# Hybrid SGU and sparse-attention block: the PV result copied in four quarter pieces and added on GpSimd before it is turned

## What is computed

```python
qi, ki, wi -> idx_score; top-256 keys per query row, chunk-causal
scores = einsum('bqhd,bqkd->bhqk', q, k_sel) * scale - slopes * |q - k|
p = softmax(where(valid, scores, NEG))
y = einsum('bhqk,bqkd->bqhd', p, v_sel)              # 8 heads of 64, one shared k and v
ob = rmsnorm(y.reshape(b, s, 8, 64), gb)
mixed = concat([oa * silu(a_z), ob * silu(b_z)])
x = x + einsum('bse,ed->bsd', mixed, w_out)
```

## Time and profile before

| | |
|---|---|
| median of 3 runs | 593.01 us (591.93 to 594.25) |
| the profiled execution: own time, span | 593.83 us, 592.0 us |
| PE busy | 560.3 us, 95% |
| DVE, ACT, POOL busy | 448.8, 372.1, 158.1 us |
| mean granted PE clock | 0.983 |

### The profile page before, as it was taken

The page is one execution under the profiler, slowest core; times in us unless marked ns, Lnnn a source line. Parts: engine busy times, 40 slices in busy tenths (PEclk is TensorE's granted clock), DMA queues, the critical chain, the costliest instruction groups (busy, mean ns, idle before and its releaser), DMA issues.

```text
span 592.0 us, 9061 instructions
## 1 busy us (share of the span) xinstructions
PE 560.3 (95%) x3038; PEld 478.4 (81%) x3038; DVE 448.8 (76%) x1134; ACT 372.1 (63%) x711; POOL 158.1 (27%) x252
## 2 busy tenths in 40 slices
PE   8999999999999999999997987999989899999987
PEld 7997888788788888878886876778878788888876
DVE  4885878998789989998792568888787878657631
ACT  5866777669976767889873546646545455555510
POOL 2750000124299966662200002012020010102020
PEclk9999999999999999999997996999989999999999
DMA  8723100112311121212122352020202001020122
GB/s 232 251 73 90 35 19 20 35 55 89 106 51 40 37 54 37 90 37 55 53 77 84 102 182 90 19 81 28 90 19 86 22 29 46 16 72 2 37 70 71
DMA packets 39981, 39.68 MB, mean 67 GB/s; under 512 B 6144, under 2 KB 28160, under 8 KB 39936
## 3 DMA queue, kind: packets, MB, share of 16 engines
q1 hardware_dynamic: 38896, 39.11, 21.8%
q10 hardware_dynamic: 1040, 0.00, 0.1%
HBM read 30.72 MB, written 8.39 MB: 66 GB/s over the span
## 4 chain that ended last, share of the span: by engine, by line
PE 76%; DVE 15%; ACT 3%; issue 3%; POOL 1%; DMA 1%; DVEq 0%; POOLq 0%; ACTq 0%
PE ps_proj L1041 37%; PE ps_proj L1207 11%; PE ps_proj L1177 5%; PE ps_lg L1069 5%; PE ps_lg L1068 5%; PE ps_tp L1162 4%; PE ps_lg L1207 2%; DVE w_lo L1347 2%; DVE cand L1439 2%; PE ps_tp L1200 1%; DVE lo_f L1648 1%; PE ps_lg L1018 1%; DVE rank L1428 1%; DVE xT_lo L1658 1%; PE ps_tp L1058 1%
## 5 line engine op out<-in xcount | busy, mean ns | idle before, releaser
L1041 PE MATMUL ps_proj<-w_hi,xT_hi 128*128 128x512 f32 (+1 forms) x432 | 165.1, 382 | 2.1 <-DVE w_lo L1347 2.1
L1041 PE MATMUL ps_proj<-w_lo,xT_hi 128*128 128x512 f32 (+1 forms) x432 | 161.8, 375 | 0.0
L1041 PE MATMUL ps_proj<-w_hi,xT_lo 128*128 128x512 f32 (+1 forms) x432 | 161.6, 374 | 0.0
L889 ACT ACTIVATE ps_lg<-score,cand 128x768 f32<-128x768 f32 (+2 forms) x96 | 95.9, 999 | 10.2 <-DVE cand L1439 10.2
L1041 PEld LDWEIGHTS ps_proj<-w_hi,xT_hi 128*128 128x128 f32 x432 | 81.9, 190 | 15.5 <-DVE w_lo L1347 3.1
L1041 PEld LDWEIGHTS ps_proj<-w_lo,xT_hi 128*128 128x128 f32 x432 | 81.8, 189 | 15.1
L1041 PEld LDWEIGHTS ps_proj<-w_hi,xT_lo 128*128 128x128 f32 x432 | 82.0, 190 | 12.3
L943 ACT CAST xT_hi<-ps_tp 128x512 fp32r<-128x512 f32 (+3 forms) x96 | 43.9, 483 | 69.6 <-PE ps_tp L1162 69.3
L1658 DVE TENSOR_TENSOR xT_lo<-ps_tp,xT_hi 128x512 fp32r<-128x512 f32 (+3 forms) x96 | 50.8, 553 | 35.0 <-ACT xT_hi L943 34.6
L711 POOL TENSOR_TENSOR yz<-hi_f,lo_f 128x512 f32<-128x512 f32 x8 | 10.3, 1286 | 189.8 <-DVE hi_f L1675 142.1
L1162 PE MATMUL ps_tp<-ident,lo_f 128*128 128x128 f32 x288 | 45.1, 279 | 10.8 <-DVE hi_f L1675 6.1
(11 more groups left out here) (173 smaller groups left out, 1127.1 us busy)
## 6 DMA issues: line engine op xcount, KB each, us to landing
stage<-in_w_in_dram SPq DMA_DIRECT2D x48, 256.0 KB, 2.7
x_in<-in_x_dram SPq DMA_DIRECT2D x8, 512.0 KB, 5.8
lo_f<-in_x_dram SPq DMA_DIRECT2D x7, 512.0 KB, 4.1
out_dram<-lo_f SPq DMA_DIRECT2D x7, 512.0 KB, 3.5
q_scratch<-nat SPq DMA_DIRECT2D x8, 256.0 KB, 2.0
q_in<-q_scratch SPq DMA_DIRECT2D x8, 256.0 KB, 3.5
stage<-in_w_out_dram SPq DMA_DIRECT2D x8, 256.0 KB, 2.6
z_scratch<-nat SPq DMA_DIRECT2D x8, 256.0 KB, 2.0
```

The lines of the kernel that those rows point to most:

```text
L889: act.activation(ps_lg[i % 2][:, 0:keys(t)], score[:, sc_off[t]:sc_off[t] + keys(t)], ACT.Sign, bias=cand[:, t:t + 1].bitcast(F32), scale= ...
L1041: mm = pe.matmul(ps_proj[u % 2][:, 0:n], a[:, k, rows], b[:, k, 0:n], start=(k == 0 and i == 0), stop=(k == KB - 1 and i == 2))
```

## The change

The copy becomes four: for odd and even heads and for the high and the low half, 64 partitions by 256 columns each, so that head pairs lie on 128 partitions. POOL adds the two halves (`add_parts`), and PE transposes two head pairs with the identity, 128 columns each, in place of four `fold` matmuls of 64. `fold` goes. `STEPS` moves one output block from h = 6 to h = 5, ahead of `turn_y`, and `mT` stands ahead of the (now no) blocks of h = 6.

```diff
-        yT = place("yT", [P, 4, P], F32, at=top[0])
+        yT = place("yT", [P, 2, P], F32)
+        y_parts = place("y_parts", [P, 2, 2, P], F32, at=top[0])
-            pool.tensor_tensor(fold[:, :], ident[:, 0:DH], ident[:, DH:P], ALU.add).then_inc(fold_ready, 1)
-            for t in range(T):
+            def add_parts(t, half):
+
+                n = 2 * t + half
+                pool.wait_ge(y_parts_done, n + 1)
+                if n > 0:
+                    pool.wait_ge(yT_done, n)
+                pool.tensor_tensor(yT[:, :, :], y_parts[:, 0, :, :], y_parts[:, 1, :, :],
+                                   ALU.add).then_inc(yT_added, 1)
+
+            for t in range(T):
+                add_parts(t, 0)
+                add_parts(t, 1)
                 finish_b(t)
-            def copy_yT(t, half):
+            def split_y(t, half):
 
                 n = 2 * t + half
                 act.wait_ge(pv_done, 2 * (n + 1))
                 if n > 0:
-                    act.wait_ge(yT_done, n)
-                act.copy(yT[:, :, :], pv_bank(n).rearrange("p (h s) -> p h s", h=4)).then_inc(yT_copied, 1)
+                    act.wait_ge(yT_added, n)
+                heads = pv_bank(n).rearrange("p (h s) -> p h s", h=4)
+                for odd in range(2):
+                    for low in range(2):
+                        last = act.copy(y_parts[HALF * odd:HALF * (odd + 1), low, :, :],
+                                        heads[HALF * low:HALF * (low + 1), odd:4:2, :])
+                last.then_inc(y_parts_done, 1)
...
-                    pe.wait_ge(yT_copied, j // 2)
+                    pe.wait_ge(y_parts_done, j // 2)
             def turn_y(t, half):
 
                 n = 2 * t + half
-                pe.wait_ge(yT_copied, n + 1)
+                pe.wait_ge(yT_added, n + 1)
                 bank = tp(("y", t, half))
-                if n == 0:
-                    pe.wait_ge(fold_ready, 1)
-                for h in range(4):
-                    mm = pe.matmul(bank[:, DH * h:DH * (h + 1)], yT[:, h, :], fold[:, :], start=True, stop=True)
+                for pair in range(2):
+                    mm = pe.transpose(bank[:, P * pair:P * (pair + 1)], yT[:, pair, :], ident[:, :])
                 mm.then_inc(yT_done, 1)
-            STEPS = {7: 3, 0: 3, 1: 2, 2: 2, 3: 2, 4: 2, 5: 1, 6: 1}
+            STEPS = {7: 3, 0: 3, 1: 2, 2: 2, 3: 2, 4: 2, 5: 2, 6: 0}
+                    if h == MIX_AT and t > 0:
+                        mT(t - 1, 0)
+                        mT(t - 1, 1)
                     for _ in range(steps):
                         next(pending, None)
                     if h == MIX_AT and t > 0:
-                        mT(t - 1, 0)
-                        mT(t - 1, 1)
                         pending = out_steps(t - 1)
```

More of the change, by code:

```diff
@@ L184, in hybrid_block @@
         ident = place("ident", [P, P], F32)
-        fold = place("fold", [P, DH], F32)
         nat = place("nat", [P, 2, BANK], F32)
@@ L326, in hybrid_block @@
         succ_ready = sem("succ_ready")
-        fold_ready = sem("fold_ready")
-        yT_copied = sem("yT_copied")
+        y_parts_done = sem("y_parts_done")
+        yT_added = sem("yT_added")
         yT_done = sem("yT_done")
@@ L589, in _ @@
                                pattern=[[-1, P]], channel_multiplier=1).then_inc(ident_ready, 1)
-            pool.wait_ge(ident_ready, 1)
-            pool.tensor_tensor(fold[:, :], ident[:, 0:DH], ident[:, DH:P], ALU.add).then_inc(fold_ready, 1)
             pool.memset(nhalf[:, :], -0.5).then_inc(setup_step, 1)
@@ L985, in _ @@
                     if h == 0 and t > 0:
-                        copy_yT(t - 1, 1)
+                        split_y(t - 1, 1)
                     if h == 4:
-                        copy_yT(t, 0)
+                        split_y(t, 0)
                     hi_pT(t, h)
@@ L995, in _ @@
                         y_square(t - 1)
-            copy_yT(T - 1, 1)
+            split_y(T - 1, 1)
             y_square(T - 1)
```

## The result

| | before | changed |
|---|---|---|
| median of 4 runs, us | 592.47 (590.04 to 594.25) | 606.48 (604.59 to 608.43) |
| ratio, 95% interval | | 1.0237 (1.0205 to 1.0269) |
| profiled execution: own time, span, us | 593.83, 592.0 | 608.05, 606.0 |
| mean granted PE clock | 0.983 | 0.977 |

What follows compares the result with a forecast made beforehand. The prediction took a chain over ACT and DVE to bound most turns, not PE. Its turn-by-turn terms, from -0.7 to +3.5 us, summed to +10.4 us, giving 603.4 us on the median of 593.01; range 594.5 to 609.

Steps and rivals of the forecast that it cites:

- What bounds: At most of the 16 turns a chain over ACT and DVE to `y_rows` decides, not PE, though PE is 95% busy.
- The sign that was to tell: At t = 7, `y_rows` starting at 4.4 us from PV's end, as before, would prove the prediction wrong.
- The price on ACT: Four copies ahead of `pT`: 0.41 us each without overlap, 1.16 us more per turn; with full overlap 0.64 more.
- The gain on PE: Two transposes in place of eight passes give back 0.62 us a turn, at most 9.9 us over 16 turns.
- n = 0 and 1: The first two turns, where projections fill PE and DVE waits for the turn: -0.7 us together.
- n = 12: One of four turns at h = 5, t >= 4 (n = 8, 10, 12, 14): about +0.7 us each, 0.47 to 1.16.
- n = 9: The turn at h = 1 of t = 5, where PE already waits for DVE: late by the full 1.16 us.
- n = 7: The turn at h = 1 of t = 4, where PE already waits for DVE: late by the full 1.16 us.
- The waits that were to show it: PE's waits for `y_rows`: about 2 us at h = 5, 3.4 and 2.7 at h = 1; another before the last turn.
- Overlap: Rival: the four ACT copies overlap, so the delay is 0.64 us a turn, +2.8 in all, 595.8 us; chance 0.16.
- PE decides: Rival: the 0.62 us come through at all 16 turns, 593.0 - 9.9 = 583.1 us; chance 0.11.
- The clock case: Rival: up to six more clock falls at n = 3, 9 and h = 5 turns, up to 609.4 us; chance 0.18.

Runs made afterwards that it cites:

- e3: The kernel before with the copy cut into four pieces of 64 partitions by 256 columns, no POOL add, fold turn and old order kept: 611.08 us beside 592.63.
- e5: The changed kernel with only the two copies of v's high part, POOL adding the high part to itself: 594.27 us beside 591.97 for the kernel before.
- e9: The kernel before with only the turn shortened to two transposes, halves not added and two heads left out: 590.91 us beside 593.40.
- e4: The changed kernel with the four copies behind the copies of `pT` at the same step: 604.23 us beside 592.63 for the kernel before.
- e10: The changed kernel with two DVE moves and, for t >= 4, two pieces ahead of the `pT` copies and two behind: 597.52 us beside 593.40 before.
- e11: The changed kernel with two DVE moves and, for t >= 4, all four pieces behind the `pT` copies: 599.36 us beside 593.40 before.

## Why the prediction was right, and where it was off

- **What bounds.** Right, and now shown: most turns are decided by the chain over ACT and DVE. e3 gives it from one side, e5 and e9 from the other. The sign that was to tell came: `y_rows` at t = 7 is 5.37 us behind the first copy in place of 4.33.
- **The price on ACT.** I chose non-overlapping copies with 0.41 a piece and 1.16 us more in the chain. A piece is 0.366, the next starts 0.38 behind it, and the chain is 1.05 longer. The choice between the two ends was right: nothing overlaps. The Trainium skill's 93 ns (ScalarE: Activation LUTs, What ACT_TABLE_LOAD costs) would have given 0.7, and this measurement differs from it.
- **The gain on PE.** The ceiling of 9.9 us and its absorption hold: e9 gives 2.5. But the -0.3 and -0.4 at n = 0 and 1 were too good by 0.2 and 0.9. At n = 1 the step that failed is "here DVE waits for the turn". DVE's `lo_pT` waits for ACT's late copy of `pT`, `y_rows` starts 3.81 us behind the first copy in place of 3.36, and PE waits for it where it had no such wait. That is the whole 0.45 by which the stretch is longer; timeline of the changed kernel:

```profile
351.02 0.43 DVE L1671 TENSOR_TENSOR xT_lo<-ps_tp,xT_hi 128x256 fp32r<-128x256 f32 x1 [0.66 <-ACT xT_hi L952]
...
353.48 0.63 PE L1072 MATMUL ps_tp<-ident,q_in 128*128 128x128 f32 x4 [1.12 <-DVE hi_f L1688]
```

- **Turn by turn, and the clock.** The sum of the sixteen was 10.4 and is 11.7. The largest miss is n = 12, 1.9 against 0.7, then n = 1 and n = 9 (1.7 against 1.2). At n = 9 and n = 12 it is the clock. I had put such falls into a rival and not into the sum. PE waits 1.92 us at n = 9 and 1.35 at n = 12, and the stretch behind runs at half rate, where the kernel before has 1.00; timeline and busy time by stretch of the changed kernel, beside the earlier trace rows:

```profile
473.71 0.48 PE L1176 MATMUL ps_tp<-ident,lo_f 128*128 128x128 f32 x1 [1.92 <-DVE hi_f L1688]
...
492.63 0.44 PE L1176 MATMUL ps_tp<-ident,lo_f 128*128 128x128 f32 x2 [1.37 <-DVE hi_f L1688]
...
528.20 0.90 PE L1176 MATMUL ps_tp<-ident,lo_f 128*128 128x128 f32 x3 [1.35 <-DVE hi_f L1688]
```

```profile
474.00:476.00 2.00, 2.00 (x9) 1.81 (x9) 1.55 (x4) 1.30 (x3) 1.02 (x1) 0.50 0.00 0
...
528.00:530.00 2.00, 1.80 (x6) 1.61 (x7) 1.09 (x3) 0.86 (x2) 0.00 (x0) 0.55 0.00 0
```

  What such a fall costs can be estimated. At n = 10 and n = 14, turns of the same kind as n = 12 with waits of 1.37 and 1.40 us and no fall, the stretch is 0.7 longer, so the fall at n = 12 cost about 1.2. At n = 9 `y_rows` restarts PE 1.04 later and a wait further on shrinks from 1.01 to 0.44, which leaves 0.5 of the 1.7: again 1.2. Without the two falls the sum is about 9.3. So the turns cost about 1 us less than forecast and the falls 2.4 more, and that the two sums lie so near is in part luck. The length of the wait doesn't tell by itself where the clock falls: 1.35 us was followed by a fall, 1.37 and 1.40 were not, nor 2.35 at n = 3.
- **n = 7** was overestimated, 1.16 against 0.7. PE's restart is 1.03 later than before, but the wait that followed it before, 0.32 for `lo_pT`, is gone in the changed kernel, and this leaves 0.71. Both kernels have a fall of the clock behind this turn. Timeline of the kernel before, then of the changed one:

```profile
433.74 1.09 PE L1058 MATMUL ps_tp<-ident,q_in 128*128 128x128 f32 x4 [0.32 <-DVE xT_lo L1658]
```

```profile
439.30 0.37 PE L1176 MATMUL ps_tp<-ident,lo_f 128*128 128x128 f32 x1 [2.68 <-DVE hi_f L1688]
```

- **Left out:** the turn's own wait for its bank, 1.6 us in four places in the changed kernel and 4.3 in e3. In the changed kernel it lies inside the same lateness, since `y_rows` still starts 1.04 later there.
- **The waits that were to show it.** At h = 1 of t = 4, 3.4 us were expected and 2.68 seen, with 0.47 ahead of the turn; at h = 1 of t = 5, 2.7 expected and 1.92 seen, with 0.29 ahead of the turn. At n = 15 1.3 was expected, and 1.00 seen, because the pieces are shorter than taken:

```profile
581.87 0.44 PE L1202 MATMUL ps_tp<-ident,yT 128*128 128x128 f32 x2 [1.00 <-POOL yT L726]
```

- **The rivals.** Overlap and "PE decides" are refuted by the copies' starts and by e9. The clock case is half true: two more falls in the profiled execution, at two of its six places. Its figure with three falls, 606.4, is as good as the measured 606.48, but that agreement isn't shown to be more than chance.

Open is how the 14.0 us of the medians divide between turns and clock falls, since executions of one kernel differ in the falls, and whether the time ahead of the first turn changed at all. A hint: the one run of the changed kernel with a mean granted clock of 0.983 took 604.91 us, and five runs of the kernel before with 0.983 took 593.83 to 595.76. At an equal clock the change cost 9 to 11 us, so some 4 of the 14.0 may be the clock; this is one run.

## What to carry to other kernels

Work taken from the busiest engine is worth only what the next link lets through: before costing a gain, look for that engine's waits right behind the place, and measure the gain alone (here 2.5 of 9.9 us) before paying for it. An instruction on a lightly loaded engine (ACT 63%) can be the dearest of all if the path to the next wait runs through it. The old copy lay almost entirely in a pause that ACT had anyway: it held ACT for 0.48 us, and in e4, with nothing ahead of the copy of `pT`, ACT pauses 2.86 us there in place of 2.42, so 0.44 longer (timeline of e4 at h = 4 of t = 7, below). Of what the four pieces added beyond that, 1.04 us reached `y_rows` at half of the turns. If pieces must be copied, a division is worth trying: ahead of the critical copy those that fit the pause, the rest behind. e10 is the best of the places tried, though not clear of e11.

```profile
560.37 1.07 ACT L952 CAST xT_hi<-ps_tp 128x512 fp32r<-128x512 f32 x2 [2.86 <-PE ps_tp L1176]
561.33 1.51 ACT L965 COPY y_parts<-ps_proj 64x256 f32<-64x256 f32 x4
```

## What the runs showed of the hardware

Copies of 64 partitions by 256 columns from PSUM on ACT take 0.366 us each and start 0.375 apart, with no overlap among them and none with the copy of 128 partitions that follows (1.50 for four, next start at 1.53), whether they change partitions (the changed kernel) or keep them (e3, 1.51 and 1.53). A copy of 128 partitions overlaps its successor by 0.1 us. Why is not shown.
